# Hybrid decoder step on one Trainium2 core: 38 instead of 28 expert products computed ahead of the expert loop

## The chip, the cores and the metric

The kernel runs on one core of one Trainium2 chip. The metric is the device time of one execution in microseconds (us); lower is better. A core has TensorE (PE; PEld are its weight loads), VectorE (DVE), ScalarE (ACT), GpSimd (POOL) and SyncE (SP), which here only issues DMAs. The engines run their own instruction streams and meet through semaphores.

## What is computed

One layer of a decoder for 512 prompt tokens and 32 sample tokens (8 sequences of 4), width 1024. The part that the change touches is the second half, PEER, a mixture over 16,384 tiny experts:

```python
q = (x @ w_query).reshape(T, PEER_HEADS, 2, PEER_KEY_HALF)
scores = jnp.einsum('thpd,hpnd->thpn', q, sub_keys)
s_top, i_top = lax.top_k(scores, PEER_TOPK)              # 16 of 128, per head and key half
cand = s_top[:, :, 0, :, None] + s_top[:, :, 1, None, :]
best, sel = lax.top_k(cand..., PEER_TOPK)                # 16 experts per head and token
gates = jax.nn.softmax(best, axis=-1)
act = gelu(einsum('td,tkd->tk', xb, expert_u[ib]))
out = einsum('tk,tkd->td', gates * act, expert_v[ib])
```

What stands before it (a gated delta rule, a multi-scale pool, the projections) is the same in both kernels.

## The kernel before, in words

For the first 384 tokens (`TD`, three tiles of 128) the experts are computed densely. The 16,384 experts are 128 blocks of 128. For block `b` the kernel forms `gelu(U_b h)` for all 384 tokens, multiplies it by a matrix of gates that is zero for the experts that a token did not choose, and adds the product with `V_b` to accumulators in PSUM. The other 160 tokens (the fourth prompt tile and the samples) are computed sparsely: each chosen expert's row is fetched from memory by an indirect DMA (`fetch`, 320 of 128 rows of 4 KB, issued by POOL into a ring of `RING` = 8 buffers) and DVE does the dot products (`sparse`).

Every product is in two-term precision. A weight chunk of 128 x 1024 (512 KB) is loaded by SP (`load_chunk`, L432) into `w_raw`; ACT writes its rounded part `w_hi` (`split_hi`, L437), and DVE (`split_lo`, L441) or POOL (`early_low`, L2244) the remainder `w_lo`. Then PE does three matmuls for each of 8 slices: hi x hi, hi x lo, lo x hi. Each of `w_raw`, `w_hi`, `w_lo` and the PSUM tile `pp` has two buffers.

The program of this part has four stages, each written out by hand for each engine.

- **Queries and scores.** 16 query chunks; DVE finds the top 16 of each score row (`top16`). After the last one DVE makes the *choice* for the samples and then for the sparse tile (`choice(p)`, p = 0 and 1 use the tiles that `ORDER` names), and PE has no query left.
- **The head.** Beside that choice PE does early products: U-products of blocks listed in `EARLY`, with `early_pieces(pe, n)` (one piece is one slice, three matmuls, L2227). ACT applies the gelu (`early_gelu`), SP stores the result to memory (`early_d`, 192 KB each, `store_early`). Before, PE does `E_QUERY` = 4 products, then the *turns* (`TURNS`: ten tiles transposed or broadcast in 20 half-turns of four 128 x 128 matmuls, L2531 to L2541, copied out by ACT at L2675 and stored by SP at L2399), then products 4 to 9 (`E_HEAD` = 10), and then `turn(0)`, which transposes the choice of the first dense tile (L2563). POOL issues its first eight fetches in one run between the turns and product 4.
- **The one-hots.** The gate matrix is built by 96 *quads*, 32 for each of the three dense tiles (`quads(u)`): DVE, POOL and ACT together write 16 one-hot matrices `hot_a`, `hot_b` for a quad ahead (`HOTS` = 4 quads may be in flight), PE multiplies four of them (L2552), ACT copies the result (`gstage`, L2712). DVE works on the choice of the next tile beside the first three sets. After each quad PE does some pieces of early products (`E_PIECES`), 18 products in all before the change.
- **The expert loop.** For `b` = -2 to 127 PE does `u_product(b + 2)` (24 matmuls, L2584), unless block b + 2 is in `EARLY`, and `v_product(b)` (18 matmuls, L2597). For an early block SP loads the stored result back (`load_early`, L2435, into two buffers `ge_e`). SP loads `v_raw` (L2427) as soon as DVE has split the block two before (L3045), and a gate tile (`gt`) for every four blocks.

The constants that set the order are

```python
NE = 28
EARLY = [1 + 9 * i // 2 for i in range(NE)]
E_QUERY, E_HEAD, LOW_LAG = 4, 10, 5
n_quads = ND * TQ
e_upto = [(NE - E_HEAD) * KC * min(q + 1, n_quads - 2) // (n_quads - 2) for q in range(n_quads)]
E_PIECES = [b - a for a, b in zip([0] + e_upto, e_upto)]
```

with ND = 3, TQ = 32, KC = 8.

Of the kernel before, what the change touches and what calls it, by code (L numbers as in the profile page):

```python
# [14 lines left out]
P = 128  # L15
D = 1024
KC = D // P
# [55 lines left out]
NE = 28  # L73
EARLY = [1 + 9 * i // 2 for i in range(NE)]
# [90 lines left out]
def build(nc, x_in, c_in, vec_in, cst_in, wba_in, ada_in, stream_in, v_in, urow_in, conv_in, pool_in, delta_in,  # L165
          wpool_in, keys_in, wout_in, y_out, conv_out, delta_p_out, delta_s_out, pool_out):
    with ExitStack() as ctx:
# [2040 lines left out]
        E_QUERY, E_HEAD, LOW_LAG = 4, 10, 5  # L2208
# [134 lines left out]
        with nc.Block() as block:  # L2343
            @block.gpsimd
            def _(pool):
# [35 lines left out]
            def _(sp):  # L2381
# [12 lines left out]
                for n, (kind, t) in enumerate(TURNS):  # L2394
                    if kind == "own":
                        continue
                    sp.wait_ge(turned_out, 2 * n + 2)
                    rows = TS if (kind, t) in (("x", NC), ("row", 1)) else P
                    sp.dma_start(turned_d[n, 0:rows], turn_sb[n % 4][0:rows]).then_inc(turn_st[n % 4], 16)  # L2399
# [6 lines left out]
                for i in range(E_QUERY, E_HEAD):  # L2406
                    load_chunk(sp, Chunk(C_EARLY + i + 4))
                    store_early(sp, i)
# [76 lines left out]
            def _(pe):  # L2485
# [31 lines left out]
                early_pieces(pe, E_QUERY * KC)  # L2517


                pe.wait_ge(sc_read, 2 * H + 2)  # L2520
                for n, (kind, t) in enumerate(TURNS):
                    for half in range(2):
                        if 2 * n + half >= 3:
                            pe.wait_ge(turned_out, 2 * n + half - 2)
                        bank = banks[(2 * n + half) % 3]
                        for q in range(4):
                            k = 4 * half + q
                            at = slice(q * P, (q + 1) * P)
                            if kind == "x":
                                rows = P if t < NC else TS  # L2530
                                last = nc.tensor.transpose(bank[0:rows, at], x[:, k, t * P:t * P + rows], ident)  # L2531
                            elif kind == "row":
                                pe.wait_ge(repeated, 2 * KC)
                                g = ((mod[:, G2 + k, 0:1].to_broadcast([P, P]), P), (g2_rep[:, k, :], TS),
                                     (v_("gf")[:, k:k + 1].to_broadcast([P, P]), P))[t]
                                last = nc.tensor.matmul(bank[0:g[1], at], g[0], ident, start=True, stop=True)
                            elif t == 0:
                                pe.wait_ge(h2_whole, KC)
                                last = nc.tensor.transpose(bank[:, at], h2[:, k, SPARSE_P * P:(SPARSE_P + 1) * P], ident)
                            else:  # L2540
                                last = nc.tensor.transpose(bank[:, at], h2_rep[:, k, :], ident)  # L2541
                        last.then_inc(turned, 1)
# [83 lines left out]
            def _(act):  # L2626
# [10 lines left out]
                for k in range(2 * H):  # L2637
# [7 lines left out]
                    if k:  # L2645
                        keep(k - 1)
# [502 lines left out]
```

## Time and profile before

| | before |
|---|---|
| median of 3 runs | 1984.91 us (1983.94 to 1985.22) |
| the profiled execution | 1984.22 us |
| its span | 1982.3 us |
| PE / DVE / ACT / POOL busy, share of the span | 95% / 79% / 43% / 37% |
| head (first early product to `turn(0)`) | 749.90 to 817.27 us |
| one-hots | 817.27 to 1017 us |
| expert loop | 1017 to 1962 us |

A span is the time from the first to the last instruction of the profiled execution; 1.9 us lie around it. "Busy" of PE is the share of time in which some matmul is between its start and its modelled end; since matmuls overlap, a PE that is 100% busy can still wait a little, so the chain of waits is read beside it. Every duration below is from this one execution.

### The profile page before, as it was taken

The numbers are of one execution on the slowest core, as the hardware profiler recorded it, in microseconds if no ns is written. First come the engines' busy times: TensorE is split into PE (matmuls) and PEld (weight loads), VectorE is DVE, ScalarE is ACT, GpSimd is POOL, SyncE is SP. The second block draws the span as 40 slices with busy tenths as digits, with TensorE's granted clock in tenths as the row PEclk, the third lists the DMA queues.
The fourth block names the chain that finished last, engine by engine and source line by source line (L and its number), as shares of the span: only waits on it lengthen the run. The fifth ranks groups of instructions, "written<-read, shape, count | busy, mean of one in ns | idle before, by whom it ended". The sixth has DMA issues, their size and how long they took to land.

```text
span 1982.3 us, 33646 instructions
## 1 busy us (share of the span) xinstructions
PE 1892.7 (95%) x12681; PEld 1706.5 (86%) x12681; DVE 1557.0 (79%) x3017; ACT 855.3 (43%) x1473; POOL 743.0 (37%) x575
## 2 busy tenths in 40 slices
PE   5989999999999998888899999999999999999997
PEld 3679999999977898878888989898889898989886
DVE  4476777777666788999957888888888887988887
ACT  3344444444433235699963333333333333333333
POOL 0010000000025433789833444444445455545462
PEclk8999999999999998999999999999999999999999
DMA  8822222222272325467688999999999998999974
GB/s 359 325 60 81 70 70 70 81 70 67 68 289 86 128 65 176 153 194 222 183 263 311 351 342 364 351 358 350 341 357 358 354 336 341 359 331 355 344 277 145
DMA packets 173247, 466.06 MB, mean 235 GB/s; under 512 B 16032, under 2 KB 72704, under 8 KB 169760
## 3 DMA queue, kind: packets, MB, share of 16 engines
q1 hardware_dynamic: 127008, 296.13, 42.6%
q0 software_dynamic: 46080, 167.79, 22.9%
q8 instruction: 102, 1.67, 0.4%
q14 instruction: 57, 0.47, 0.1%
HBM read 422.24 MB, written 41.62 MB: 234 GB/s over the span
## 4 chain that ended last, share of the span: by engine, by line
PE 52%; DVE 11%; issue 2%; ACT 1%; POOL 1%; DVEq 0%; ACTq 0%
PE pp L2584 21%; PE dd L2597 18%; PE pp L2597 9%; PE dd L2552 2%; PE pp L2227 2%; DVE top_i L2270 1%; DVE top_i L2259 1%; DVE less L2260 1%; POOL hot_a L2371 1%; DVE hot_b L2818 1%; DVE top L2796 1%; DVE top_v L2265 1%; DVE top_v L2254 1%; PE pp L453 1%; DVE cand L2906 1%
## 5 line engine op out<-in xcount | busy, mean ns | idle before, releaser
L437 ACT ACTIVATE w_hi<-w_raw 128x1024 fp32r<-128x1024 f32 x202 | 212.6, 1052 | 142.2 <-PE pp L453 102.8
L2584 PE MATMUL pp<-act_hi,w_hi 128*128 128x384 f32 x792 | 268.6, 339 | 1.7 <-DVE acc L3053 1.7
L2584 PE MATMUL pp<-act_lo,w_hi 128*128 128x384 f32 x792 | 266.9, 337 | 0.0
L2584 PE MATMUL pp<-act_hi,w_lo 128*128 128x384 f32 x792 | 266.2, 336 | 0.0
L453 PE MATMUL pp<-act_hi,w_hi 128*128 128x272 f32 x1056 | 239.5, 308 | 9.2 <-DVE act_lo L758 4.4
L441 DVE TENSOR_TENSOR w_lo<-w_raw,w_hi 128x1024 fp32r<-128x1024 f32 x177 | 215.8, 1220 | 25.4 <-ACT w_hi L437 25.4
L453 PE MATMUL pp<-act_lo,w_hi 128*128 128x272 f32 x1056 | 218.7, 288 | 0.0
L453 PE MATMUL pp<-act_hi,w_lo 128*128 128x272 f32 x1056 | 218.7, 289 | 0.0
L2752 ACT ACTIVATE co_hi<-cf 128x384 fp32r<-128x384 f32 x128 | 67.4, 526 | 350.6 <-PE pp L2597 310.8
L453 PEld LDWEIGHTS pp<-act_hi,w_hi 128*128 128x128 f32 x1056 | 164.4, 190 | 26.0 <-issue 17.9
L2299 POOL DMA_INDIRECT x<-in_v,idx x80 | 138.3, 1729 | 122.8 <-DVE acc L2978 114.5
L2371 POOL TENSOR_SCALAR hot_a<-cst,gcols 128x128 f32<-128x128 f32 x144 | 174.8, 1226 | 16.3 <-PE dd L2552 14.5
L3045 DVE TENSOR_TENSOR v_lo<-v_raw,v_hi 128x1024 fp32r<-128x1024 f32 x128 | 156.5, 1223 | 28.2 <-ACT v_hi L2754 26.3
L453 PEld LDWEIGHTS pp<-act_lo,w_hi 128*128 128x128 f32 x1056 | 166.7, 189 | 0.0
L453 PEld LDWEIGHTS pp<-act_hi,w_lo 128*128 128x128 f32 x1056 | 165.9, 189 | 0.0
L2299 POOL DMA_INDIRECT x<-in_urow,idx x80 | 99.6, 1245 | 172.8 <-DVE junk L2970 156.7
L2597 PE MATMUL dd<-v_hi,co_hi 128*128 128x512 f32 x512 | 159.9, 393 | 1.5 <-DVE v_lo L3045 1.5
L2760 ACT ACTIVATE ge<-pp 128x384 f32<-128x384 f32 x100 | 49.2, 492 | 258.2 <-PE pp L2584 255.0
L2597 PE MATMUL dd<-v_lo,co_hi 128*128 128x512 f32 x512 | 158.8, 391 | 0.0
L2597 PE MATMUL dd<-v_hi,co_lo 128*128 128x512 f32 x512 | 158.8, 391 | 0.0
L2584 PEld LDWEIGHTS pp<-act_hi,w_hi 128*128 128x128 f32 x792 | 148.8, 188 | 7.2 <-issue 3.5
L2584 PEld LDWEIGHTS pp<-act_lo,w_hi 128*128 128x128 f32 x792 | 148.8, 188 | 4.5
(437 smaller groups left out, 4335.8 us busy)
## 6 DMA issues: line engine op xcount, KB each, us to landing
w_raw<-in_stream SPq DMA_DIRECT2D x206, 512.0 KB
v_raw<-in_v SPq DMA_DIRECT2D x128, 512.0 KB
ada_w<-in_ada SPq DMA_DIRECT2D x24, 1024.0 KB, 11.7
gt<-gate_matrix SPq DMA_DIRECT2D x31, 768.0 KB
gate_matrix<-gstage SPq DMA_DIRECT2D x11, 2048.0 KB, 10.1
early<-cst SPq DMA_DIRECT2D x28, 192.0 KB, 4.0
cst<-early SPq DMA_DIRECT2D x28, 192.0 KB
wrow<-in_wout SPq DMA_DIRECT2D x8, 512.0 KB, 8.3
```

Source lines behind the costliest of these rows:

```text
L437: nc.scalar.activation(w_hi[k.slot][:], w_raw[k.slot][:], ACT.Copy).then_inc(w_hi_done, 1)
L441: nc.vector.tensor_tensor(w_lo[k.slot][:], w_raw[k.slot][:], w_hi[k.slot][:].bitcast(F32), ALU.subtract).then_inc(w_lo_done, 1)
L453: last = nc.tensor.matmul(pp[s][:, b, 0:HN], w[:, c * P:(c + 1) * P], a[:, c, b * HN:(b + 1) * HN], start=(c == 0 and w is w_hi[s] and a i ...
L2227: last = nc.tensor.matmul(pp[s][:, 0, 0:TD], w[:, c * P:(c + 1) * P], a[:, c, 0:TD], start=(c == 0 and w is w_hi[s] and a is act_hi), stop ...
L2299: nc.gpsimd.indirect_dma_start(out=ring[n % RING][:], out_offset=None, in_=tables[kind], in_offset=bass.IndirectOffsetOnAxis(ap=idx_of[whi ...
L2371: last = nc.gpsimd.tensor_scalar(hot_a[:, (q % HOTS) * 4 + o, :], iota, gcols[u % 2][:, 0, c:c + 1], gcols[u % 2][:, 2, c:c + 1], ALU.is_e ...
L2552: last = nc.tensor.matmul(dd[:, q % 4, o::4], hot_a[:, v, :], hot_b[:, v, :], start=True, stop=True)
L2584: last = nc.tensor.matmul(pp[s][:, 0, 0:TD], w[:, c * P:(c + 1) * P], a[:, c, 0:TD], start=(c == 0 and w is w_hi[s] and a is act_hi), stop ...
L2597: last = nc.tensor.matmul(accs[t][half], co[:, cols], v[:, half * 512:(half + 1) * 512], start=(b == 0 and co is co_hi[0] and v is v_hi[0] ...
L2752: nc.scalar.activation(co_hi[e % 2][:], cf[e % 2][:], ACT.Copy).then_inc(c_hi_done, 1)
L2760: nc.scalar.activation(ge[b % 2][:], pp[k.slot][:, 0, 0:TD], ACT.Gelu).then_inc(pp_read[k.slot], 1)
L3045: nc.vector.tensor_tensor(v_lo[e % 2][:], v_raw[e % 2][:], v_hi[e % 2][:].bitcast(F32), ALU.subtract).then_inc(v_lo_done, 1)
```

## The change

`NE` goes from 28 to 38, and the early blocks are spread evenly over blocks 1 to 121. `E_HEAD` goes from 10 to 14: fourteen products in one row, with the turns put between their pieces (half-turns after the third and the sixth of the eight pieces of products 1 to 10). That leaves 24 products for the one-hots, where 18 were. ACT's, SP's and POOL's programs are written in the same new order: ACT's first early gelu comes before its last copy of scores (`keep(2 * H - 1)`); POOL's eight fetches stand one behind each of the `w_lo` of products 8 to 15; SP stores one turn at the front of each step.

```diff
-NE = 28
-EARLY = [1 + 9 * i // 2 for i in range(NE)]
+NE = 38
+EARLY = [1 + (NEXP - 4) * i // NE for i in range(NE)]
...
-        E_QUERY, E_HEAD, LOW_LAG = 4, 10, 5
+        E_QUERY, E_HEAD, LOW_LAG = 4, 14, 5
+        FETCH_FROM = E_HEAD - RING
...
-                pool.wait_ge(chosen, 1)
-                pool.wait_ge(turned, 2 * TT)
-                for n in range(4):
-                    fetch(pool, n)
-                pool.wait_ge(turned, 2 * len(TURNS))
-                for n in range(4, RING):
-                    fetch(pool, n)
                 for i in range(E_QUERY, E_HEAD):
                     early_low(pool, Chunk(C_EARLY + i + 2))
+                    if i >= FETCH_FROM:
+                        n = i - FETCH_FROM
+                        if n == 0:
+                            pool.wait_ge(chosen, 1)
+                            pool.wait_ge(turned, 2 * TT)
+                        if n == 4:
+                            pool.wait_ge(turned, 2 * len(TURNS))
+                        fetch(pool, n)
...
-                for i in range(E_QUERY):
+                for i in range(E_HEAD):
+                    n = i - 1
+                    if 0 <= n < len(TURNS) and TURNS[n][0] != "own":
+                        sp.wait_ge(turned_out, 2 * n + 2)
...
+                        sp.dma_start(turned_d[n, 0:rows], turn_sb[n % 4][0:rows]).then_inc(turn_st[n % 4], 16)
                     load_chunk(sp, Chunk(C_EARLY + i + 4))
                     store_early(sp, i)
...
-                early_pieces(pe, E_QUERY * KC)
...
+                for i in range(E_HEAD):
+                    if 0 <= i - 1 < len(TURNS):
+                        early_pieces(pe, 3)
+                        half_turn(2 * (i - 1))
+                        early_pieces(pe, 3)
+                        half_turn(2 * (i - 1) + 1)
+                        early_pieces(pe, 2)
+                    else:
+                        early_pieces(pe, KC)
...
-                early_pieces(pe, (E_HEAD - E_QUERY) * KC)
                 pe.wait_ge(turned_out, 2 * len(TURNS))
                 turn(0)
...
+                early_gelu(act, 0)
                 keep(2 * H - 1)
-                for i in range(E_QUERY):
-                    early_gelu(act, i)
...
+                for i in range(1, E_HEAD):
+                    if i - 1 < len(TURNS):
+                        turned_half(2 * (i - 1))
+                        if i == 5:
+                            exponents(0)
+                        turned_half(2 * (i - 1) + 1)
+                    early_gelu(act, i)
+                    if i in (1, 2):
+                        repeats(range(KC // 2 * (i - 1), KC // 2 * i))
+                    if i == 10:
+                        exponents(1)
```

`half_turn`, `turned_half` and `repeats` hold the bodies of the loops that stood there before, unchanged but for the first wait (`sc_read`, the last copied scores), which is now inside half-turn 0.

The head on PE. Before, from the last piece of product 3 to the first of product 4 (`x`, `mod`, `h` and the like are what is turned):

```order
L2227 MATMUL pp<-act_hi,w_lo 128x384
L2531 MATMUL dd<-cst,x 128x128 x32
L2531 MATMUL dd<-cst,x 32x128 x8
L2536 MATMUL dd<-cst,mod 128x128 x8
L2536 MATMUL dd<-cst,g_rep 32x128 x8
L2536 MATMUL dd<-cst,vec 128x128 x8
L2539 MATMUL dd<-cst,h_166 128x128 x8
L2541 MATMUL dd<-cst,h_rep 128x128 x8
L2227 MATMUL pp<-act_hi,w_hi 128x384
```

After, the first two half-turns, inside product 1 (the three lines of a piece stand three times between them):

```order
L2228 MATMUL pp<-act_hi,w_lo 128x384
L2528 MATMUL dd<-cst,x 128x128 x4
L2228 MATMUL pp<-act_hi,w_hi 128x384
L2228 MATMUL pp<-act_lo,w_hi 128x384
L2228 MATMUL pp<-act_hi,w_lo 128x384
L2228 MATMUL pp<-act_hi,w_hi 128x384
L2228 MATMUL pp<-act_lo,w_hi 128x384
L2228 MATMUL pp<-act_hi,w_lo 128x384
L2228 MATMUL pp<-act_hi,w_hi 128x384
L2228 MATMUL pp<-act_lo,w_hi 128x384
L2228 MATMUL pp<-act_hi,w_lo 128x384
L2528 MATMUL dd<-cst,x 128x128 x4
```

The eighty matmuls of the turns, which stood in one block, are twenty groups of four with nine or fifteen matmuls of products between them.

The first quads on PE, before:

```order
L2563 MATMUL pp<-cst,picks 128x128 x4
L2552 MATMUL dd<-hot_b,hot_a 128x128 x4
L2227 MATMUL pp<-act_hi,w_hi 128x384
L2227 MATMUL pp<-act_lo,w_hi 128x384
L2227 MATMUL pp<-act_hi,w_lo 128x384
L2552 MATMUL dd<-hot_b,hot_a 128x128 x4
L2227 MATMUL pp<-act_hi,w_hi 128x384
L2227 MATMUL pp<-act_lo,w_hi 128x384
L2227 MATMUL pp<-act_hi,w_lo 128x384
L2227 MATMUL pp<-act_hi,w_hi 128x384
L2227 MATMUL pp<-act_lo,w_hi 128x384
L2227 MATMUL pp<-act_hi,w_lo 128x384
```

and after:

```order
L2559 MATMUL dd<-hot_b,hot_a 128x128 x4
L2228 MATMUL pp<-act_hi,w_hi 128x384
L2228 MATMUL pp<-act_lo,w_hi 128x384
L2228 MATMUL pp<-act_hi,w_lo 128x384
L2228 MATMUL pp<-act_hi,w_hi 128x384
L2228 MATMUL pp<-act_lo,w_hi 128x384
L2228 MATMUL pp<-act_hi,w_lo 128x384
L2559 MATMUL dd<-hot_b,hot_a 128x128 x4
```

Where one and two pieces took turns, nearly every quad now has two.

POOL between the queries and the one-hots, before:

```order
L2244 TENSOR_TENSOR w_lo<-w_raw,w_hi 128x1024 x10
L2299 DMA x<-in_urow,idx_129 128x1024 x4
L2299 DMA ring_122<-in_urow,idx_129 128x1024
L2299 DMA ring_123<-in_urow,idx_129 128x1024
L2299 DMA ring_124<-in_urow,idx_129 128x1024
L2299 DMA ring_125<-in_urow,idx_129 128x1024
L2244 TENSOR_TENSOR w_lo<-w_raw,w_hi 128x1024 x6
L2371 TENSOR_SCALAR hot_a<-cst,gcols_158 128x128 x48
```

and the end of that part after:

```order
L2300 DMA ring_123<-in_urow,idx_129 128x1024
L2245 TENSOR_TENSOR w_lo<-w_raw,w_hi 128x1024
L2300 DMA ring_124<-in_urow,idx_129 128x1024
L2245 TENSOR_TENSOR w_lo<-w_raw,w_hi 128x1024
L2300 DMA ring_125<-in_urow,idx_129 128x1024
L2373 TENSOR_SCALAR hot_a<-cst,gcols_158 128x128 x48
```

A fetch now stands between POOL's last `w_lo` and its first one-hot.

## Rows read from the trace of the kernel before

**Rows 1.** The page's busy time: engine, us, share of span, instructions

```profile
PE 1892.7 (95%) x12681; PEld 1706.5 (86%) x12681; DVE 1557.0 (79%) x3017; ACT 855.3 (43%) x1473; POOL 743.0 (37%) x575
```

**Rows 2.** Busy time by stretch: window, length, engines, granted clock, DMA share, GB/s

```profile
750.00:818.00 68.00, 60.64 (x348) 57.56 (x348) 61.44 (x275) 35.64 (x65) 32.22 (x19) 0.92 0.62 207
818.00:1016.00 198.00, 171.76 (x1201) 163.25 (x1201) 180.28 (x510) 181.58 (x428) 176.21 (x145) 0.97 0.64 188
1050.00:1850.00 800.00, 800.00 (x3967) 719.76 (x3966) 671.49 (x854) 280.72 (x386) 378.31 (x283) 1.00 0.94 348
...
1750.00:1800.00 50.00, 50.00 (x248) 44.86 (x248) 43.99 (x46) 18.59 (x26) 26.10 (x18) 1.00 0.98 362
1850.00:1950.00 100.00, 98.27 (x485) 86.95 (x484) 82.24 (x85) 35.08 (x49) 64.22 (x30) 1.00 0.77 287
```

**Rows 3.** The chain that ended last, expert loop: start us, us, what

```profile
1208.73 4.22 PE pp L2584 x24
1212.95 2.76 PE dd L2597 x12
1215.71 1.36 PE pp L2597 x6
```

**Rows 4.** Waits of engines, 1050 to 1900: us in total, times, longest

```profile
PE pp L2584 <- DVE acc L3053: 0.9, 1, 0.9
```

**Rows 5.** Waits of SP's queue, 1050 to 1900

```profile
SPq L2427 <- DVE v_lo L3045: 585.0, 114, 8.2
```

**Rows 6.** DMA, 1100 to 1800: packets and rate; issues of SP

```profile
DMA packets 67739, 245.90 MB, mean 351 GB/s; under 512 B 7670, under 2 KB 10366, under 8 KB 67693
...
v_raw<-in_v SPq DMA_DIRECT2D x94, 512.0 KB
w_raw<-in_stream SPq DMA_DIRECT2D x74, 512.0 KB
...
cst<-early SPq DMA_DIRECT2D x21, 192.0 KB
```

**Rows 7.** Instructions in order of time, PE, the head: start us, us, [idle before <-releaser]

```profile
749.90 0.44 PE L2227 MATMUL pp<-act_hi,w_hi 128*128 128x384 f32 x1
...
760.56 0.46 PE L2227 MATMUL pp<-act_hi,w_hi 128*128 128x384 f32 x1 [1.96 <-POOL w_lo L2244]
...
770.64 1.47 PE L2531 MATMUL dd<-cst,x 128*128 128x128 f32 x12
775.42 6.14 PE L2531 MATMUL dd<-cst,x 128*128 128x128 f32 x28 [3.31 <-ACT turn_sb L2675]
...
783.75 1.94 PE L2536 MATMUL dd<-cst,g_rep 128*32 128x128 f32 x16
...
817.27 0.63 PE L2563 MATMUL pp<-cst,picks 128*128 128x128 f32 x4 [1.41 <-DVE picks L2926]
```

**Rows 8.** The same of ACT, the head

```profile
756.36 0.60 ACT L2631 ACTIVATE scores<-dd 128x512 f32<-128x512 f32 x1 [6.63 <-DVEq L2794]
...
758.09 1.28 ACT L2240 ACT_TABLE_LOAD   x1
```

**Rows 9.** The same of POOL, end of the head

```profile
817.11 2.35 POOL L2244 TENSOR_TENSOR w_lo<-w_raw,w_hi 128x1024 fp32r<-128x1024 f32 x1 [0.79 <-ACT w_hi L437]
819.45 8.58 POOL L2371 TENSOR_SCALAR hot_a<-cst,gcols 128x128 f32<-128x128 f32 x9
```

**Rows 10.** The chain that ended last, one-hots

```profile
868.56 1.06 PE pp L2227 x6
869.62 0.89 PE dd L2552 x8
```

**Rows 11.** Groups of instructions by line, 818 to 1016: busy us, mean ns

```profile
L441 DVE TENSOR_TENSOR w_lo<-w_raw,w_hi 128x1024 fp32r<-128x1024 f32 x18 | 22.3, 1240 | 4.7 <-ACT w_hi L437 4.7
L437 ACT ACTIVATE w_hi<-w_raw 128x1024 fp32r<-128x1024 f32 x18 | 19.0, 1058 | 3.9 <-PE pp L2227 3.8
L2240 ACT ACTIVATE cst<-pp 128x384 f32<-128x384 f32 x18 | 8.6, 476 | 0.0
```

**Rows 12.** Waits of engines, 818 to 1016

```profile
PE dd L2552 <- ACT hot_a L2698: 15.6, 14, 2.1
```

More of the change, by code:

```diff
@@ L2516, in _ @@
                 score(2 * H - 1)
-                early_pieces(pe, E_QUERY * KC)
[L2520 to L2542, printed above, removed]
@@ new lines, in half_turn @@
+                def half_turn(m):
+                    n, half = m // 2, m % 2
+                    kind, t = TURNS[n]
+                    if m == 0:
+                        pe.wait_ge(sc_read, 2 * H + 2)
+                    if m >= 3:
+                        pe.wait_ge(turned_out, m - 2)
+                    bank = banks[m % 3]
+                    for q in range(4):
+                        k = 4 * half + q
+                        at = slice(q * P, (q + 1) * P)
+                        if kind == "x":
+                            rows = P if t < NC else TS
+                            last = nc.tensor.transpose(bank[0:rows, at], x[:, k, t * P:t * P + rows], ident)
+                        elif kind == "row":
+                            pe.wait_ge(repeated, 2 * KC)
+                            g = ((mod[:, G2 + k, 0:1].to_broadcast([P, P]), P), (g2_rep[:, k, :], TS),
+                                 (v_("gf")[:, k:k + 1].to_broadcast([P, P]), P))[t]
+                            last = nc.tensor.matmul(bank[0:g[1], at], g[0], ident, start=True, stop=True)
+                        elif t == 0:
+                            pe.wait_ge(h2_whole, KC)
+                            last = nc.tensor.transpose(bank[:, at], h2[:, k, SPARSE_P * P:(SPARSE_P + 1) * P], ident)
+                        else:
+                            last = nc.tensor.transpose(bank[:, at], h2_rep[:, k, :], ident)
+                    last.then_inc(turned, 1)
@@ L2669, in _, with turned_half @@
+                def turned_half(m):
+                    n, half = m // 2, m % 2
+                    kind, t = TURNS[n]
                     rows = TS if (kind, t) in (("x", NC), ("row", 1)) else P
-                    if kind != "own" and n >= 4:
+                    if kind != "own" and n >= 4 and half == 0:
                         act.wait_ge(turn_st[n % 4], 16 * (n // 4))
                     to = own_of[t] if kind == "own" else turn_sb[n % 4]
-                    for half in range(2):
-                        act.wait_ge(turned, 2 * n + half + 1)
-                        nc.scalar.activation(to[0:rows, half * 512:(half + 1) * 512], banks[(2 * n + half) % 3][0:rows],
-                                             ACT.Copy).then_inc(turned_out, 1)
@@ L2677, in _ @@
-                    if n == 3:
-                        exponents(0)
+                    act.wait_ge(turned, m + 1)
+                    nc.scalar.activation(to[0:rows, half * 512:(half + 1) * 512], banks[m % 3][0:rows],
+                                         ACT.Copy).then_inc(turned_out, 1)
+                for i in range(1, E_HEAD):
[9 more added lines that the diff above has]
+                        exponents(1)
@@ L2714, in store_row @@
                                          ACT.Copy).then_inc(quad_read, 1)
-                for i in range(E_QUERY, E_HEAD):
-                    early_gelu(act, i)
-                    if i == E_QUERY:
-                        exponents(1)
                 for s in range(4):
```

27 lines of the change are left out of this document (10 added, 17 removed).

## The prediction

> **What bounds the kernel now.** I read four views in this order. The busy times by stretch first [rows 2]: in the expert loop, 1050 to 1850 us, PE is busy 800.00 of 800.00 us at full clock, while the one-hots (818 to 1016) leave it idle 26 of 198 us and there DVE (180 us), ACT (182) and POOL (176) are nearly as full as PE (172). The page's 95% for PE [rows 1] is the average over such unlike stages. Second, the chain that ended last: in the loop it is PE alone, piece after piece, 4.22 us for a U-product and 2.76 + 1.36 = 4.12 us for a V-product [rows 3]. Third, the waits there: PE's whole list from 1050 to 1900 is one wait of 0.9 us [rows 4]. SP's queue in that stretch waits 585 us for DVE to free a `v_raw` [rows 5]: loads are issued when their buffer comes free, so the transfers are not late now. But DMA is close behind: share 0.94 at 348 GB/s over 800 us [rows 2]. So the loop's time is its number of products: 100 x 4.22 + 128 x 4.12 = 949 us, about what it takes.
>
> **A. Ten U-products leave the loop.** Ten times 4.22 us [rows 3] of PE, nothing beside it: **-42.2 us** if everything else keeps up. DVE and ACT each lose ten splits there, and their load does not rise to PE's: DVE is busy 671 of 800 us [rows 2]; ten splits of 1.24 us [rows 11] fewer over the loop make it about 661 of 765, 86%.
>
> DMA is the doubt. From 1100 to 1800 it moved 245.9 MB for 94 blocks of V, 74 of U and 21 stored gelus [rows 6]. With 38 early blocks in 124 instead of 28 in 126, 94 blocks have about 7.5 fewer loads of U (512 KB) and 7.5 more of a stored gelu (192 KB): 245.9 - 7.5 x 0.33 = 243.4 MB in 700 - 7.5 x 4.22 = 668 us, 364 GB/s against 351. The share grows in the same ratio, 0.94 to 0.975. The trace has one stretch like that: 1750 to 1800, 362 GB/s at share 0.98, with PE busy for all of its 50 us [rows 2]. So it fits, barely. Near full, some load will come late, above all where the tiles for the end are read on top. I take 3 us of new PE waits in the loop, near to that stretch's nothing, with 0 as the lower end. The upper end: nothing moves faster than the present 348 GB/s. In the 800 us 278.4 MB were moved [rows 2]; less 8.4 x 0.33 = 2.8 MB that is 275.6 MB and 792 us, a gain of 8 us there, and of some 7 us in the other 150 us, where the share falls to 0.77: 15 us of the 42, so +27. **Term +3 (0 to 27).**
>
> **B. The head: four more products, turns inside.** The first early product starts at 749.90 and `turn(0)` runs at 817.27, after 67.4 us [rows 7], and just then waits 1.41 us for DVE's `picks`. So PE and DVE end the head almost together now, and PE gets 16.9 us more. PE's own work after the change: 14 x 4.22 = 59.1; turned halves at full clock 0.49 us (12 matmuls in 1.47 [rows 7]), 14 of them 6.9; the six that broadcast take 0.97 (1.94 for two), 5.8. Sum 71.8. Waits: the halves need the last scores copied, and ACT now has the first gelu ahead of that. Product 0 ends at 754.1; then `w_hi` 1.06, the table load 1.28 [rows 8], gelu 0.48 [rows 11], and both copies of scores, about 0.9: 757.8. PE reaches half-turn 0 at 755.7, so it waits some 2.1 us. That takes the place of the 1.96 us before 760.56 [rows 7]. About 2 us go for twenty changes from a product to a turn and back, and 1.6 for matmuls at the lower clock behind the wait (before, products 2 and 3 took the 10.08 us from 760.56 to 770.64 [rows 7] instead of 8.44; the granted clock of the head is 0.92 on average [rows 2]). End: 749.9 + 71.8 + 2.1 + 2 + 1.6 = 827.4, against 817.3. The wait of 3.31 us for ACT before 775.42 [rows 7] and the slow halves behind it pay for the rest of the 16.9 us.
>
> DVE is not later than that: it had `picks` ready at 817.2; POOL makes one or two more `w_lo` beside its choice, at 2.35 us [rows 9] if each stopped it for its whole length, so 822. The exponents of the second choice are done on ACT behind product 10, near 812, before DVE asks. POOL's `w_lo` of product 15 follows the end of product 13 by 1.06, then 2.35, then one fetch; its first one-hot comes some 2.7 us after the columns instead of 0.8 [rows 9], but DVE, which sets the pace of the first quads, is not held by it. That makes 10.1, and I add 0.4 for POOL's lateness: **term +10.5.** Lower end +5 (no wait at all, 71.8 us of work), upper end +17 (none of the four products hidden).
>
> **C. The one-hots: 24 products for 18.** PE gets 6 x 4.22 = 25.3 us. Its own work: a quad 0.89, two pieces 1.06 [rows 10]; before 96 x 0.89 + 144 x 0.53 = 162 us of 198, now 96 x 0.89 + 192 x 0.53 = 187. ACT gets 6 x (1.06 + 0.48) = 9.2 us on its 182, DVE 6 x 1.24 = 7.4 on its 180 [rows 2, 11]. No engine alone would pass 198, so the lower end is 0. But they wait for each other in every quad (PE for ACT's one-hots 15.6 us [rows 12]), and ACT's 191 us at the efficiency it has now, 182 of 198, is 208. With PE also at 95% of the old length I expect less efficiency, not more. The upper end is all of PE's 25. I take **+10**, what ACT's row gives, nearer to the row of the fullest engine than to PE's whole addition.
>
> **D. The rest.** Behind the loop (1962 to the end) nothing changes. The stored gelus in the head and one-hots add 10 x 0.7 MB in 266 us at shares of 0.62 and 0.64 [rows 2]; eight fetches spread out instead of in one burst. Nothing.
>
> Sum: -42.2 + 3 + 10.5 + 10 = -18.7 us on the profiled execution's 1984.2, that is 1965.5; the median of the runs is 0.7 above that execution, so 1966.
>
> **The rivals.**
> 1. *The loop becomes a matter of transfers, and the kernel slower.* The mechanism is term A's upper end: if DMA moves no more than the 348 GB/s of now, `v_raw` and `w_raw` land after PE wants them, -42.2 turns into -15, and with B and C (+20.5) the kernel takes 1990. It decides from the point where the loop needs more than DMA can give: 364 against 348. For it: a share of 0.94 leaves little. Against: 362 GB/s in [rows 2]'s fullest stretch without a PE wait, and the 585 us in which SP waits for buffers, not for transfers [rows 5]. Chance 0.10.
>    A milder form is a cap somewhere between. At 358 GB/s the 275.6 MB take 770 us where PE needs 765, so with the uneven demand from block to block some 10 us instead of 3, and 1973; this lies in my forecast's own range. The Trainium skill ("DMA: Bandwidth & Descriptors", Specifications) gives about 358 GB/s as the HBM limit per core, which would speak against 364 being reached; the 50 us at 362 GB/s here differ, so the measurement decides.
> 2. *PE becomes the bound of the one-hots.* Every engine is above 88% there and a late one delays all. Then C is +25 and the sum -3.4: 1981; with the head at its upper end too, 1987. For it: DVE's `w_lo` stands five quads behind a product whose successor now comes after four rather than five. Against: DVE and ACT run up to four quads ahead. Chance 0.15.
> 3. *It all hides.* The head at +6, the one-hots at +3, the transfers at 0: 1951. For it: PE idles 26 us in the one-hots. Chance 0.10.
> 4. *The change does not do what it says* (the turns inside the products force the clock down or stop ACT, so that the head alone costs 25 us more than forecast): 1990. The half-turns are a sixth of PE's work there. Chance 0.03.
>
> **How the numbers follow.** The forecast has 0.62, with its own range 1957 to 1976: the head within 4, the one-hots within 6, the loop 0 to 10. For a range that holds 8 in 10 I reach to 1955 below, leaving out half of rival 3, and to 1984 above, taking in rival 2 without the late head. About 0.2% (4 us) is what a measurement of this kernel can tell from no change; faster is then below 1981, slower above 1989. Faster: forecast 0.62, rival 3 0.10, and a third of rival 2: 0.77. Slower: 0.11 (rivals 1 and 4, most of each). The same: 0.12.
>
> **What would show it.** Right: in the new profile about 908 to 915 us of loop with PE's waits below 10 us; DMA's share near 0.98 at 360 GB/s or more; `turn(0)` near 827 and no longer waiting for `picks`, but DVE waiting there some 6 us for the transposed columns; one-hots of about 208 us. Wrong: PE waiting in the loop for `v_lo` or `w_lo` behind DMA landings, in tens of us (rival 1); a PE without idle time in the one-hots and more than 215 us of them (rival 2); or a `turn(0)` beyond 834.

## The result, and the profile after

The changed kernel takes **1970.44 us** (median of 4 runs, 1969.34 to 1972.14), the kernel before 1984.66 in the same comparison: a ratio of 0.9931, 95% interval 0.9919 to 0.9943. That is 14 us faster, between 11 and 16. The forecast was 1966 in a range of 1955 to 1984: right in its direction and range, with 4 us less gain than forecast. The profiled execution, which all rows below are from, took 1972.14 us with a span of 1970.2; it was the longest of the four, and against the profiled execution of before it gains 12.1 us of span.

The busy times by stretch, in the columns of [rows 2]. The third row is the one-hots from `turn(0)` to the first product behind the last quad:

```profile
750.00:818.00 68.00, 65.37 (x409) 62.89 (x408) 62.86 (x274) 38.23 (x71) 35.04 (x17) 1.00 0.60 194
818.00:1016.00 198.00, 179.88 (x1212) 174.07 (x1211) 176.50 (x490) 168.30 (x382) 170.61 (x133) 0.97 0.66 191
827.00:1046.80 219.80, 198.55 (x1356) 192.56 (x1356) 189.31 (x517) 192.23 (x442) 184.81 (x147) 0.97 0.67 194
1050.00:1850.00 800.00, 800.00 (x3942) 716.48 (x3941) 682.99 (x871) 283.48 (x391) 390.23 (x286) 1.00 0.96 360
1500.00:1550.00 50.00, 50.00 (x243) 44.13 (x243) 44.41 (x52) 18.68 (x26) 25.53 (x19) 1.00 1.00 381
```

And the same stretch of the one-hots before, from its own `turn(0)` on:

```profile
817.30:1016.90 199.60, 173.26 (x1213) 164.51 (x1213) 181.15 (x511) 181.92 (x429) 176.91 (x145) 0.97 0.64 187
```

The chain in the loop is the same as in [rows 3], in its columns:

```profile
1205.11 4.22 PE pp L2590 x24
1209.33 2.76 PE dd L2603 x12
1212.09 1.37 PE pp L2603 x6
```

The loop still has PE busy in 800.00 of 800.00 us, now with DMA at share 0.96 and 360 GB/s for 0.94 and 348 [rows 2], and in one stretch of 50 us (1500 to 1550) at 381. SP's queue waits there for DVE to free a `v_raw`, from 1050 to 1900, for 667.8 us, more than the 585.0 of [rows 5]:

```profile
SPq L2424 <- DVE v_lo L3060: 667.8, 119, 8.3
```

In the one-hots PE is busy 198.55 - 173.26 = 25.3 us longer, exactly six products, while its idle time went from 26.3 only to 21.3. In the head the granted clock is 1.00 (2.4 GHz) for 0.92. PE's waits in the head and in the loop, 1050 to 1900 (in the columns of [rows 4], which had one wait of 0.9 there):

```profile
PE dd L2528 <- ACT scores L2640: 2.1, 1, 2.1
PE pp L2570 <- DVE picks L2941: 0.6, 1, 0.6
...
PE pp L2590 <- DVE acc L3068: 1.7, 2, 0.9
```

With these I cut the span in three at PE's instructions: the head from the first early product to `turn(0)`, the one-hots to the first product behind the last quad, and the loop with what follows it to the end of the span (so 1016.9 to 1982.3 before). All times in this table are differences of starts in PE's timeline; PE's idle time in the one-hots is the window's length less its busy time. The later rows are those of the experiments below.

| kernel (early products: head + one-hots) | first early product | head | one-hots | PE idle in them | loop | span |
|---|---|---|---|---|---|---|
| before (10 + 18) | 749.9 | 67.4 | 199.6 | 26.3 | 965.4 | 1982.3 |
| changed (14 + 24) | 752.4 | 74.6 | 219.9 | 21.3 | 923.4 | 1970.2 |
| e1 (14 + 18) | 751.0 | 75.9 | 199.4 | 27.9 | 948.4 | 1974.7 |
| e2 (12 + 24) | 751.8 | 76.5 | 218.0 | 18.9 | 931.5 | 1977.9 |
| e3 (14 + 24, pieces ahead of the quads) | 755.5 | 75.2 | 213.7 | 16.8 | 923.4 | 1967.8 |
| e4 (e1, 44 pieces repeated) | 750.7 | 75.9 | 217.4 | 21.4 | 948.4 | 1992.5 |
| e5 (e2, `w_lo` in small on POOL) | 749.6 | 67.3 | 216.6 | 21.8 | 931.5 | 1965.0 |
| e6 (14 + 30) | 752.9 | 76.3 | 239.5 | 17.0 | 897.5 | 1966.2 |
| e7 (e3, three `w_lo` on DVE, turns later) | 751.7 | 71.5 | 213.3 | 16.8 | 923.4 | 1959.9 |
| e8 (e7, 14 + 30) | 749.9 | 71.5 | 230.4 | 12.5 | 897.2 | 1948.9 |
| e9 (e7, 14 + 38) | 752.0 | 71.5 | 258.4 | 7.2 | 863.1 | 1945.0 |
| e10 (e7, 14 + 46) | 749.4 | 71.5 | 289.2 | 7.6 | 829.0 | 1939.2 |

The change: +2.5 in the stages ahead of the first product, which it does not touch, +7.2 in the head, +20.2 in the one-hots, -42.0 in the loop, together -12.1. The forecast had +10.5, +10 and -39.2. The first column runs from 749.4 to 755.5 over kernels with the same code ahead of it, so single spans are compared here stage by stage, and whole times by medians. The head varies too: 74.6 to 76.3 us in the five kernels with the same program in it (changed, e1, e3, e4, e6), and the account of the head below says why.

### The profile page after: what moved, and what is told of

It is laid out like the page before. It is cut to its first block, busy times and chain, and to the rows that moved or that the text cites. A ratio compares the mean times of both kernels' runs of the same rounds, so it can differ in the third digit from the quotient of the medians.

```text
span 1970.2 us, 33663 instructions
## 1 busy us (share of the span) xinstructions
PE 1891.4 (96%) x12681; PEld 1709.6 (87%) x12681; DVE 1560.5 (79%) x3013; ACT 857.0 (43%) x1473; POOL 758.3 (38%) x579
## 4 chain that ended last, share of the span: by engine, by line
PE 52%; DVE 11%; POOL 1%; issue 1%; ACT 1%; DVEq 0%; ACTq 0%
PE pp L2590 19%; PE dd L2603 18%; PE pp L2603 9%; PE pp L2228 3%; PE dd L2559 3%; POOL hot_a L2373 1%; DVE top_i L2271 1%; DVE top_i L2260 1%; DVE less L2261 1%; DVE top L2811 1%; DVE top_v L2255 1%; DVE top_v L2266 1%; DVE cand L2921 1%; PE pp L453 1%; DVE hot_b L2833 1%
## 5 line engine op out<-in xcount | busy, mean ns | idle before, releaser
L2590 PE MATMUL pp<-act_hi,w_hi 128*128 128x384 f32 x712 | 241.5, 339 | 1.7 <-DVE acc L3068 1.7
L2590 PE MATMUL pp<-act_lo,w_hi 128*128 128x384 f32 x712 | 239.9, 337 | 0.0
L2590 PE MATMUL pp<-act_hi,w_lo 128*128 128x384 f32 x712 | 239.3, 336 | 0.0
L441 DVE TENSOR_TENSOR w_lo<-w_raw,w_hi 128x1024 fp32r<-128x1024 f32 x173 | 211.5, 1223 | 25.1 <-ACT w_hi L437 25.1
L2767 ACT ACTIVATE co_hi<-cf 128x384 fp32r<-128x384 f32 x128 | 67.4, 526 | 350.1 <-PE pp L2603 295.3
L2373 POOL TENSOR_SCALAR hot_a<-cst,gcols 128x128 f32<-128x128 f32 x144 | 180.9, 1266 | 27.3 <-PE dd L2559 25.7
L453 PEld LDWEIGHTS pp<-act_hi,w_hi 128*128 128x128 f32 x1056 | 165.8, 191 | 25.3 <-issue 17.8
L2300 POOL DMA_INDIRECT x<-in_v,idx x80 | 130.9, 1637 | 98.4 <-DVE acc L2993 90.8
L453 PEld LDWEIGHTS pp<-act_lo,w_hi 128*128 128x128 f32 x1056 | 168.3, 191 | 0.0
L1001 POOL COPY conv_new<-cbuf 128x3 f32<-128x3 f32 x24 | 8.1, 337 | 386.8 <-ACT cbuf L1200 386.8
L2300 POOL DMA_INDIRECT ring<-in_v,idx x80 | 114.3, 1429 | 91.9 <-DVE acc L2993 80.1
L2300 POOL DMA_INDIRECT ring<-in_urow,idx x80 | 102.8, 1285 | 105.7 <-DVE junk L2985 102.6
```

The source lines that it names most:

```text
L441: nc.vector.tensor_tensor(w_lo[k.slot][:], w_raw[k.slot][:], w_hi[k.slot][:].bitcast(F32), ALU.subtract).then_inc(w_lo_done, 1)
L453: last = nc.tensor.matmul(pp[s][:, b, 0:HN], w[:, c * P:(c + 1) * P], a[:, c, b * HN:(b + 1) * HN], start=(c == 0 and w is w_hi[s] and a i ...
L2300: nc.gpsimd.indirect_dma_start(out=ring[n % RING][:], out_offset=None, in_=tables[kind], in_offset=bass.IndirectOffsetOnAxis(ap=idx_of[whi ...
L2373: last = nc.gpsimd.tensor_scalar(hot_a[:, (q % HOTS) * 4 + o, :], iota, gcols[u % 2][:, 0, c:c + 1], gcols[u % 2][:, 2, c:c + 1], ALU.is_e ...
L2590: last = nc.tensor.matmul(pp[s][:, 0, 0:TD], w[:, c * P:(c + 1) * P], a[:, c, 0:TD], start=(c == 0 and w is w_hi[s] and a is act_hi), stop ...
L2767: nc.scalar.activation(co_hi[e % 2][:], cf[e % 2][:], ACT.Copy).then_inc(c_hi_done, 1)
```

## The experiments

**e1: six fewer beside the one-hots.** `NE` is 32 and all else as changed.

```diff
-NE = 38
+NE = 32
```

> NE = 32: the head of the change (14 products in a row, turns inside), but 18 products beside the one-hots as before, so six U-products go back into the expert loop. Lengths are read as: head, from the first early product to turn(0) (before 67.4 us, change 74.4); one-hots, from turn(0) to the product behind the last quad (199.9 and 220.1); loop, from there to the end of the span (965.2 and 923.1). Theory P (in the one-hots PE's waits for the others stay as long as they were, so the time of a further product there is PE's own 4.22 us, less what the third tile's set can hide): one-hots 200 to 202, loop 923.1 + 25.3 = 948.4, head 74.4; 5 us over the change, 1975. Rival O (the price of a further product is what it adds on DVE and ACT) says the same here. Rival H (the new head itself, with POOL's fetches late, is what lengthens the one-hots): they stay at 210 or more, and the kernel is at 1985.

Measured: 1979.52 us (median of 5; before 1985.68 in this comparison), ratio 0.9964 (0.9951 to 0.9977). One-hots 199.4 us, as before the change, with the same 18 products; loop 948.4, six products at 4.17 us above the changed kernel's. Rival H is out: the new head does not lengthen the one-hots. The terms add up: the head costs 7 to 9 us for four products and the one-hots 20.5 for six. Six products beside the one-hots hide 25.3 - 20.5 us, no more. The stages add up to the profiled execution's time; the median is some 4 us above the sum that I had written down.

**e2: two fewer in the head.** `E_HEAD` is 12 and `NE` 36, the fetches two to a product.

```diff
-        E_QUERY, E_HEAD, LOW_LAG = 4, 14, 5
-        FETCH_FROM = E_HEAD - RING
+        E_QUERY, E_HEAD, LOW_LAG = 4, 12, 5
+        FETCH_FROM = E_HEAD - RING // 2
```

> NE = 36, E_HEAD = 12: two products fewer in the head (POOL issues its eight fetches two by two behind the last four w_lo), 24 beside the one-hots as in the change. Theory PE-head (the head is as long as PE's work): head 74.4 - 8.4 = 66, loop 923.1 + 8.4 = 931.5, the kernel as the change, 1970. Rival DVE-head (DVE's choice beside POOL's w_lo sets the head, and PE is only as late as DVE): two w_lo fewer give back at most 2 x 2.3 us, head 70 to 72, and the kernel is 4 to 6 us slower than the change, 1975.

Measured: 1976.66 us (6 runs), ratio 0.995 (0.9938 to 0.9961). The head did not get shorter: 76.5 us. PE's waits in it:

```profile
PE pp L2570 <- DVE picks L2941: 9.8, 1, 9.8
PE dd L2528 <- ACT scores L2640: 2.1, 1, 2.1
```

The two products that left are now a wait of 9.8 us for DVE's `picks`. So DVE's choice sets the end of the head, and PE, in the changed kernel, reaches it 0.6 us earlier. The two products are back in the loop (931.5 against 923.4) for nothing. The head was even longer than the 70 to 72 us that I had expected of this theory. Since the fetches stand two by two here, e2 alone does not say what makes the choice so long; e5 does, which has the same fetches.

**e3: pieces ahead of the first quads.** Eight pieces (one product) run between `turn(0)` and the first quad, three ahead of each later set, and as many fewer between the quads.

```diff
+        LEAD = (8, 3, 3)
...
+                    early_pieces(pe, LEAD[u])
                     quads(u)
```

> The change with its 24 one-hot products placed unevenly: 8 pieces ahead of the first quad of the first set and 3 ahead of the first quad of each other set, the other 178 spread as before. Theory P: PE now waits 5.3 us for POOL's first one-hots behind turn(0) and some 2 us at each of the two other starts of a set; the pieces fill this, so the one-hots get 4 to 7 us shorter (213 to 216), nothing else moves, and the kernel is at 1964 to 1967. Rival O: DVE and ACT have the same work and are the bound, so 0 to 1 us, 1970.

Measured: 1967.83 us (4 runs), ratio 0.9904 (0.9889 to 0.9918). The changed kernel waits 5.33 us for POOL's first one-hot; e3 does a product there and waits 2.24 for DVE (PE's timelines, first quad of the changed kernel and of e3):

```profile
826.98 0.63 PE L2570 MATMUL pp<-cst,picks 128*128 128x128 f32 x4 [0.62 <-DVE picks L2941]
832.94 1.40 PE L2559 MATMUL dd<-hot_b,hot_a 128*128 128x128 f32 x5 [5.33 <-POOL hot_a L2373]
```

```profile
830.66 0.63 PE L2573 MATMUL pp<-cst,picks 128*128 128x128 f32 x4 [1.22 <-DVE picks L2944]
837.76 1.54 PE L2562 MATMUL dd<-hot_b,hot_a 128*128 128x128 f32 x8 [2.24 <-DVE hot_a L2840]
```

One-hots 213.7 for 219.9, 6.1 us less at the same number of products. The first quad comes 7.1 us behind `turn(0)` for 6.0, and the first set of 32 quads takes 69.4 us for 76.8; the second (70.9 for 71.0) and the third (66.4 for 66.1) did not move, so the leads of three did nothing. Of the 6.1 us PE's idle time gave 4.5 (21.3 to 16.8) and its busy time 1.6 (198.6 to 196.9): behind the wait of 5.33 us the changed kernel's granted clock is 0.50 from 833 to 836 us, and its mean over the first set of quads is 0.94, in e3 0.98.

**e4: PE's work alone.** e1, and in 44 of its quads one piece's matmuls are done a second time into the same accumulation. No load, split, gelu or store is added.

```diff
...
+            if again:
+                todo.insert(0 if early[0] % KC == KC - 1 else 1, (early[0], False))
...
+                        early_pieces(pe, E_PIECES[u * TQ + q], E_PIECES[u * TQ + q] == 1)
```

> The kernel of e1 (18 products beside the one-hots), but in the 44 quads that have one piece PE does that piece's three matmuls a second time, so PE has 44 x 0.53 = 23 us more work there, and no other engine, queue or transfer has any. Leaves the U-products of these blocks wrong (a slice counted twice). Theory P: one-hots as long as in the change, 216 to 222. Rival O: one-hots as in e1, 200 to 204.

Measured: 1994.29 us (one run, profiled). One-hots 217.4 for e1's 199.4: 44 x 0.53 = 23.3 us of PE work lengthened them by 18.0, which is 77%. (By the windows PE is busy 24.5 us longer, 196.0 for 171.5, and idle 6.5 less.) Six real products (48 pieces, 25.3 us, and their splits and gelus on ACT and DVE) lengthened them by 20.5, 81%. So PE's own work makes up nearly all of it; what the products ask of ACT and DVE is at most the remaining 2.5 us, and the real products also bring 2.0 us more of PE work (25.3 for 23.3), which accounts for most of that. e4 is a single run, so a price of a microsecond for the others is not excluded.

**e5: POOL's splits in small.** e2, and POOL computes only 8 of the 1024 columns of `w_lo` for products 6 to 13. This leaves out most of the low part of their weights; all else that the engines do is that of e2.

```diff
-                    early_low(pool, Chunk(C_EARLY + i + 2))
+                    nc.gpsimd.tensor_tensor(w_lo[k.slot][:, 0:8], w_raw[k.slot][:, 0:8], w_hi[k.slot][:, 0:8].bitcast(F32),
+                                            ALU.subtract).then_inc(w_lo_done, 1)
```

> The kernel of e2 (12 products in the head, where PE waited 9.8 us for DVE's picks and the head was 76.5 us), but POOL writes only 8 of the 1024 columns of w_lo for products 6 to 13, so that its instruction is short. Leaves most of the low part of those eight products' weights out. Nothing changes on DVE itself. Theory DVE-POOL (a w_lo on POOL stops the DVE instruction that runs beside it by about 2.1 us, and DVE's choice with seven or eight such stops sets the head): six or so of the stretched DVE instructions go back to their own length, DVE's two choices take 36 to 40 us instead of 51.5, PE waits 0 to 1 us for picks, head 66 to 68 us. Rival (the choice is slow for another reason, the exponents on ACT or the late scores): head 75 us or more.

Measured: 1966.59 us (one run; before 1984.73). Head 67.3 us for e2's 76.5, and PE waits 0.4 us for `picks` instead of 9.8. The only difference is how long POOL's splits work beside DVE. The same two operations on DVE and what POOL does meanwhile, in the changed kernel (start us, us; DVE's timeline and then POOL's):

```profile
810.87 3.90 DVE L2921 TENSOR_TENSOR cand<-cand,top_f 128x512 f32<-128x512 f32 x2
...
818.87 4.03 DVE L2921 TENSOR_TENSOR cand<-cand,top_f 128x512 f32<-128x512 f32 x2
```

```profile
809.63 3.46 POOL L2245 TENSOR_TENSOR w_lo<-w_raw,w_hi 128x1024 fp32r<-128x1024 f32 x1 [1.60 <-ACT w_hi L437]
...
818.95 2.86 POOL L2245 TENSOR_TENSOR w_lo<-w_raw,w_hi 128x1024 fp32r<-128x1024 f32 x1 [0.42 <-ACT w_hi L437]
```

And in e5, where no large `w_lo` stands beside them:

```profile
801.46 1.83 DVE L2924 TENSOR_TENSOR cand<-cand,top_f 128x512 f32<-128x512 f32 x2
...
807.03 1.83 DVE L2924 TENSOR_TENSOR cand<-cand,top_f 128x512 f32<-128x512 f32 x2
```

A pair takes 1.83 us alone and 3.90 or 4.03 beside a `w_lo`: some 2.1 us more. The POOL instructions, 2.4 us elsewhere, took 3.46 and 2.86 there, so both engines lose. From the first `sums` to `turn(0)` it is 42.2 us in e5, 45.5 before and 51.0 in the changed kernel (DVE's and PE's timelines: 774.74 to 816.89, 771.81 to 817.27, 775.94 to 826.98). In e5 4.87 of the 42.2 us are a wait of DVE for ACT, whose exponents of the second choice stand behind product 10 in its program:

```profile
815.57 0.28 DVE L2935 TENSOR_REDUCE gsum<-best 128x8 f32<-128x128 f32 x1 [4.87 <-ACT best L2667]
```

So DVE's own two choices, from the first `sums` to the end of `picks`, are 37.1 us in e5 and 50.9 in the changed kernel. These 13.8 us, over nine long `w_lo` more, are 1.5 us for each on average: not each of them meets a DVE instruction that it holds for its whole length.

**e6: six more beside the one-hots.** `NE` is 44.

```diff
-NE = 38
+NE = 44
```

> NE = 44: the change with 30 products beside the one-hots instead of 24, so the loop has six U-products fewer. Theory P for the one-hots: PE's 25.3 us come on top, less 0 to 3 hidden: 242 to 245 us. For the loop: PE's work is 923.1 - 25.3 = 897.8 us; by the accounting of the prediction the stretch that moved 360 GB/s in the change has to move 370 to 373. Theory room (transfers still keep up): loop 898 to 902 and the kernel as the change, 1969 to 1972. Rival DMA (they no longer do): PE waits of 10 us and more in the loop behind v_raw or w_raw, loop 908 or more, kernel 1980 or more.

Measured: 1967.89 us (4 runs), ratio 0.9917 (0.99 to 0.9933). Loop 897.5, six products at 4.32 less, and PE without a gap at 370 GB/s:

```profile
1080.00:1850.00 770.00, 770.00 (x3777) 687.42 (x3776) 674.01 (x863) 272.25 (x373) 395.39 (x287) 1.00 0.98 370
```

The transfers have room. The one-hots grew by 19.7 for 25.3 us of products, so the exchange still pays: 25.9 - 19.7 = 6.2 us by the stages. The medians show less, some 3 us (0.9917 against 0.9931, with intervals that overlap), and the head, whose code is the same, took 1.7 us longer, for which the account of the head below has the cause.

**e7: both repairs.** e3; the turns begin one product later, so that PE has work while ACT copies the last scores; and `w_lo` of products 11, 12 and 13 is done by DVE itself, between the parts of its second choice.

```diff
+        ON_DVE = (11, 12, 13)
...
+                    if i + 2 not in ON_DVE:
+                        if i + 2 == ON_DVE[-1] + 1:
+                            pool.wait_ge(w_lo_done, Chunk(C_EARLY + i + 2).n)
...
-                    n = i - 1
+                    n = i - 2
...
+                choice(0, lambda: None)
+                choice(1, beside_second)
```

> The kernel of e3 with two things more: the turns start one product later (so that half-turn 0 doesn't wait 2.1 us for the last scores), and w_lo of products 11, 12 and 13 is written by DVE, between the steps of its second choice, instead of by POOL. Theory DVE-POOL: on DVE a w_lo takes 1.2 us, on POOL it stops DVE by 2.1, so DVE's choices lose three stops and win three instructions, 2 to 3 us shorter; with PE's 2.1 us gone the head is 72 to 73.5 us instead of 75.2, the kernel 1.5 to 3 us faster than e3. Rival (DVE is the bound and its own work counts): the three instructions lengthen the head by 3.6 us, 78 to 79, and the kernel is slower than e3.

Measured: 1961.41 us (4 runs), ratio 0.9884 (0.9867 to 0.99). The head is 71.5 us (72 to 73.5 expected) and PE has no wait left in it. DVE's two choices, with the three splits in them, take 46.0 us where they take 51.5 in e3. That is twice the 2 to 3 us expected; in the new order POOL has only six `w_lo` beside them, where it had ten. The three splits take 1.22, 1.23 and 1.23 us on DVE, and nothing beside them is stretched:

```profile
805.90 1.22 DVE L441 TENSOR_TENSOR w_lo<-w_raw,w_hi 128x1024 fp32r<-128x1024 f32 x1
807.03 1.82 DVE L2923 TENSOR_TENSOR cand<-sel_f,cst 128x512 f32<-128x512 f32 x2
808.89 1.83 DVE L2928 TENSOR_TENSOR cand<-cand,top_f 128x512 f32<-128x512 f32 x2
```

So 71.5 us is what fourteen products and twenty half-turns cost PE by themselves. The other 3.1 us of the changed head are its waits (2.1 + 0.6) and 0.4.

**e8, e9: e7 with 44 and with 52 early products.**

```diff
-NE = 38
+NE = 44
```

> e7 (lead of 8 pieces, turns one product later, three w_lo on DVE) with 44 early products instead of 38: six more leave the loop for the one-hots. Their PE time is 25.3 us in either place; the question is how much of PE's idle time in the one-hots is left to fill. There PE is busy 196.5 of e7's 213.3 us, so 16.8 are idle; the same six products took 4.3 us off the idle time when the changed kernel went from 38 to 44 (21.3 to 17.0). F (idle time still to be filled): the one-hots grow by 21 to 23 us to some 235, the loop falls by 25.9 as in e6_44_early to 897.5, the head stays at 71.5, and the kernel is 3 to 4 us under e7: 1957.5 to 1958.5. E (what is idle now is PE waiting for the first one-hots of a set and for the last gathers, which no product shortens): the one-hots grow by all of 25, the time is 1960 to 1962.

> The same with 52 early products: fourteen leave e7's loop. R (DMA still has room): the loop falls by 14 x 4.27 = 60 us to 864, the one-hots grow by 52 to 59, and the time is e7's or up to 7 us below: 1954 to 1962. T (the transfers become the bound): the loop of e6 with 44 ran at 370 GB/s and share 0.98; eight more would need about 384 GB/s and a share of 1.02. Nothing seen so far moved more than 382 GB/s over 50 us. Then PE waits in the loop, for w_raw or v_raw behind their landings on ACT, DVE or POOL, 5 to 25 us in all; the loop is 870 to 890 us, and the time 1962 to 1985. This is where the upper bound of the prediction's loop term would show, if anywhere.

Measured: e8 1951.82 us (4 runs), ratio 0.983 (0.9814 to 0.9847), and e9 1947.17 (4 runs), ratio 0.9806 (0.979 to 0.9823). Both theories for e8 were too pessimistic, and so was the one for e9 (one-hots 45.1 us above e7's, for the 52 to 59 expected): e8's one-hots grew by 17.1 us, not by 21 or more. PE's idle time took 4.3 us of the 25.3 (16.8 to 12.5), and PE's busy time grew by 21.3 (196.5 to 217.8) rather than 25.3. Of that difference 1.2 us are the quads' own 768 matmuls, 104.1 us in e7 and 102.9 in e8; the rest I did not settle. e9's loop was 863.1, as expected if PE stays the bound, and from 1110 to 1850 it moved 382 GB/s with PE busy throughout. In e9 over 100 us:

```profile
1300.00:1400.00 100.00, 100.00 (x490) 88.93 (x489) 91.57 (x137) 35.33 (x48) 52.82 (x40) 1.00 1.01 393
```

**e10: 60 early products.** `NE` is 60, every second block.

> e9 with 60 early products instead of 52, to look for the point at which the transfers (or DVE) hold the loop. e9 moved 382 GB/s at share 0.99 from 1110 to 1850, PE still busy in all of it. Eight more: R (PE stays the bound): loop 863.1 - 8 x 4.27 = 829, and the one-hots, where PE's idle time is down to 7 us, grow by 28 to 33.8 us to 287 to 292: 0 to 6 us under e9, 1941 to 1947, with some 395 GB/s in the loop. T (382 to 393 GB/s is what the transfers give): 8 x 0.33 = 2.6 MB fewer to move in the loop, which at the same rate saves only 7 us of the 34: loop 840 to 856, PE waits for landings of 10 to 25 us, and the time 1955 to 1972, slower than e9. DVE is the other suspect: busy 674 of 740 us in e9, some 94% here; then the waits would be for acc or v_lo on DVE and not behind a landing.

Measured: **1942.18 us** (4 runs, 1941.46 to 1943.94), ratio 0.9779 (0.9763 to 0.9795). The loop is 829.0, as the theory of PE had it. The busy times, and PE's only waits from 1125 to 1900:

```profile
1130.00:1850.00 720.00, 720.00 (x3482) 636.18 (x3481) 671.05 (x863) 257.23 (x351) 415.57 (x296) 1.00 1.01 396
```

```profile
PE pp L2597 <- DVE acc L3085: 1.7, 2, 0.9
```

Even at 396 GB/s no transfer holds the loop. The fastest kernel of this study is e10, 2.2% below the kernel before and 1.5% below the changed one. PE's idle time in the one-hots has stopped falling (7.2 and 7.6 us), so what is left of this exchange was not looked for further.

## Why the prediction was right, and where it was not

**Bound by PE in the loop: right.** -42.0 us for ten products in the stage (forecast -42.2). The loop is 965.4 us with 28 early products and 829.0 with 60, that is 4.26 us a product over the whole range, against 4.22 of [rows 3].

**The term of +3 for late transfers: not there.** PE's waits went from 0.9 to 1.7 us. The step "it fits, barely" took share 0.98 for a limit near at hand. The runs show that the share of before, 0.94, said little: the rate followed the demand, 348, 360, 370, 382 and 396 GB/s, at shares of 0.94, 0.96, 0.98, 0.99 and 1.01. Rival 1, the term's upper end (348 GB/s as a ceiling, +27), is refuted, and its milder form at 358 GB/s too. The Trainium skill ("HBM Reference", Specifications (TRN2)) says besides the figure per core that the prediction quoted that a core that streams alone measures well above its share, about 425 GB/s; the 396 GB/s here agree. Where the ceiling lies no run here shows.

**The head, +10.5: measured +7.2, and by another path.** The sum of PE's own work, 71.8 us, was right: e7 without waits shows 71.5. So the "about 2 us for twenty changes from a product to a turn and back" do not exist. The wait of 2.1 us for the scores came as forecast, to the tenth.

The "1.6 for matmuls at the lower clock" are absent from the changed kernel's profiled execution, but that is luck. In e1, e2, e4, e5 and e6, where PE has the same program up to there and waits the same 2.1 us, the clock fell to 1.2 GHz behind the wait; in the changed kernel and e3 it did not. Here e1 and then the changed kernel, in the 3 us from half-turn 0 on:

```profile
759.20:762.20 3.00, 3.00 (x11) 3.00 (x12) 2.74 (x20) 0.60 (x1) 0.00 (x0) 0.50 0.68 179
```

```profile
760.60:763.60 3.00, 3.00 (x20) 2.96 (x21) 2.75 (x19) 0.90 (x2) 0.00 (x0) 1.00 0.63 171
```

From half-turn 0 to half-turn 2 it is 6.6 to 6.7 us in those five, and 5.1 in the other two. What decides it no run here shows. By the timelines it reached the end of the head through DVE: POOL's `w_lo` came later and met another of DVE's copies (`top<-top_v`, 1.92 us in e1, 0.35 in the changed kernel), and the first `sums` stood 25.1 us behind the first early product in e1 and e6, 23.6 in the changed kernel and e3. So the heads are 75.9 and 76.3 us in e1 and e6 and 74.6 in the changed kernel, and in another execution the term can be +8.5 to +9.

The step that failed is "**DVE is not later than that**". It counted one or two more `w_lo` of POOL beside the choice, which would end it at 822. In POOL's timelines six stand beside the two choices before (772.05 to 812.90) and ten after (775.74 to 823.95), since the turns inside the products spread them out. `picks` came at 826.8, and PE waited for them, where the prediction had DVE waiting for PE. Of these 9.7 us after the 817.1 of before, 2.5 are from the stages ahead, 1.6 from a later first `sums` (one of DVE's copies before it takes 1.69 us beside a `w_lo`, 0.20 before), and 5.6 from the choices themselves. That `turn(0)` stands at 826.98, where 827.4 was forecast, is therefore luck as well. e2 shows that it is DVE that holds the head, e5 that it is POOL's splits that hold DVE, and e7 that the wait goes when three of them go and the choices are 5.5 us shorter. The Trainium skill ("SBUF — State Buffer", SBUF: two separate sides) has DVE and GpSimd share a port pair as an exclusive lock, for a DVE instruction with two inputs in SBUF or in a two-port mode against one of GpSimd, the later one blocked for the whole of the other; 1.83 us turning into 3.90 and 4.03 beside a POOL instruction of 2.4 agrees with it.

**The one-hots, +10: measured +20.2, the largest error.** The step that failed is the choice of ACT's row: "ACT's 191 us at the efficiency it has now" gave 208. ACT's 192.2 busy us were foreseen well, but the length of the stage does not follow the fullest engine. PE's own work was also put too low, at 162 us before and 187 after where it is busy 173.3 and 198.6. The reading that fits is that PE waits in one quad and is waited for in the next, so its added work lands on the path wherever the others are not late at that moment. It shows in who waits. Over the whole stage in the changed kernel, 827 to 1046.8, for which [rows 12] have PE's side before:

```profile
POOL hot_a L2373 <- PE dd L2559: 25.7, 31, 3.4
DVE hot_b L2833 <- PE dd L2559: 22.3, 23, 3.1
ACT gstage L2731 <- PE dd L2559: 17.4, 28, 3.8
...
PE dd L2559 <- ACT hot_a L2717: 10.6, 12, 2.1
```

and before, from 818 to 1016:

```profile
POOL hot_a L2371 <- PE dd L2552: 14.5, 18, 3.0
DVE hot_b L2818 <- PE dd L2552: 10.8, 13, 1.5
ACT gstage L2712 <- PE dd L2552: 8.9, 16, 2.4
```

The three engines together now wait 65 us for PE's quads, where it was 34, and PE 10.6 us for ACT's one-hots where it was 15.6. Rival 2 was nearer than the forecast: 20.2 of its 25. e4 gives the cause by itself, since PE's matmuls alone bring 18 of 23.3 us. Of PE's 21.3 idle us one wait, for the first one-hot, is 5.33, and no other is longer than 2.2; e3 filled the first. That wait is for POOL and was 3.87 us before: "DVE, which sets the pace of the first quads, is not held by it" was wrong too, for POOL's `w_lo` and fetch in front of its first one-hot cost PE 1.5 us.

**The sum.** -18.7 forecast, -12.1 in the profiled execution: +10.2 from the one-hots, -3.3 from the head, -2.8 from the loop, +2.5 from the stages ahead. The one-hots are rival 2 by four fifths, and the head and the loop pay for part of it: the forecast was as near as it was because its errors went both ways. By the medians the gain is 14.2 us.

## What to carry to other kernels

Where one engine bounds the kernel and a stage beside leaves it idle, moving work there gains only the idle time that the work really fills: here 5 of 25 us. Look at where each gap lies and put the work into it (one product ahead of the first quad was worth 6 us), and price work added to an engine that is busy for 87% of a stage at most of its length (here 77 to 81%; in the later steps 68, 83 and 91%), not by the busy time of the fullest neighbour. Once the gaps are placed well, try more of the same exchange: the step from 38 to 60 products, which would have looked exhausted from the first result, brought 19 us more. And a share of DMA near 0.95 with SP waiting for buffers was not yet a limit here.

## What the runs showed of the hardware that I had not expected

- DMA carried 396 GB/s over 720 us with 16 engines at share 1.01, and PE without a transfer to wait for; before the change the share was already 0.94 at 348. GB/s per unit of share rose from 370 to 392, so the share is no linear measure of what is left.
- One POOL instruction with two inputs of 1024 columns (2.4 us) costs a DVE instruction that starts beside it up to 2.1 us, even a copy of two columns; over the two choices it is 1.5 us on average. The copy `gsum<-best 128x2` took 2.07 us on DVE from 781.16, and ended when POOL's `w_lo` of 780.82 + 2.39 did. The same subtraction takes 1.23 us on DVE itself, so that to give it to POOL costs DVE more than to do it.
- Short turns between products do not lower the clock: in every kernel with the new head it is granted at 1.00 from 768 to 810 us, over some fifteen half-turns. A wait of 2.1 us of PE was followed by some 3 us at 1.2 GHz in five of seven executions with the same program on PE up to there, and in two it was not; where it came, the half-turns behind it came 1.5 to 1.6 us later.
